# Two heads' score products on the two row halves of TensorE's array, with the forget-gate sums added by a product of their own

## The reference, cut to what matters

```python
log_f = jax.nn.log_sigmoid(f_logit.astype(jnp.float32) + b_forget[l].astype(jnp.float32))
cum = jnp.cumsum(log_f, axis=1).transpose(0, 2, 1)
...
for q0 in range(0, S, Q_BLOCK):          # Q_BLOCK = 128, S = 512, 8 heads of 64 channels
    q1 = q0 + Q_BLOCK
    s = jnp.einsum('bhqd,bhkd->bhqk', q[:, :, q0:q1], k[:, :, :q1]).astype(jnp.float32) * scale
    if cum is not None:
        s = s + cum[:, :, q0:q1, None] - cum[:, :, None, :q1]
    mask = jnp.concatenate([jnp.ones((Q_BLOCK, q0), dtype=bool), diag_mask], axis=1)
    s = jnp.where(mask, s, -jnp.inf)
    p = jax.nn.softmax(s, axis=-1).astype(v.dtype)
    outs.append(jnp.einsum('bhqk,bhkd->bhqd', p, v[:, :, :q1]))
```

## Time and profile before

| what | us |
|---|---|
| median of 3 runs (1755.65 to 1756.67) | 1756.38 |
| the profiled execution, its own time | 1755.61 |
| its span in the trace | 1753.6 |
| TensorE matmul records busy | 1727.1 (98%) |
| TensorE weight loads busy | 1375.6 (78%) |
| VectorE busy | 1088.2 (62%) |
| ScalarE busy | 685.6 (39%) |
| GpSimd busy | 197.7 (11%) |

### The profile page before, as it was taken

How to read it: one execution, slowest core, us unless ns; L and a number is a source line. 1 busy time by engine, 2 the same in 40 slices (tenths; PEclk the granted TensorE clock), 3 DMA queues, 4 the chain that set the end, 5 groups by cost and what they waited for, 6 DMA issues and landing times.

```text
span 1753.6 us, 21973 instructions
## 1 busy us (share of the span) xinstructions
PE 1727.1 (98%) x7814; PEld 1375.6 (78%) x7814; DVE 1088.2 (62%) x1646; ACT 685.6 (39%) x1130; POOL 197.7 (11%) x136
## 2 busy tenths in 40 slices
PE   7999999999999999999999999999999999999998
PEld 6777777877788888888878777777778888888886
DVE  6899987766545555533349988866755555555222
ACT  5555554433343322222236554552434423332222
POOL 1720100010030000001134310000101200000010
PEclk9999999999999999999999999999999999999999
DMA  5341211333333333333342321213333333333331
GB/s 151 91 105 50 61 49 36 96 86 94 108 96 96 96 96 96 96 90 96 90 100 64 97 60 49 55 42 103 91 96 108 96 96 96 96 96 93 94 93 69
DMA packets 310004, 152.19 MB, mean 87 GB/s; under 512 B 30436, under 2 KB 309214, under 8 KB 309932
## 3 DMA queue, kind: packets, MB, share of 16 engines
q1 hardware_dynamic: 309624, 150.99, 30.7%
q10 hardware_dynamic: 308, 0.25, 0.1%
HBM read 149.09 MB, written 2.10 MB: 86 GB/s over the span
## 4 chain that ended last, share of the span: by engine, by line
PE 93%; DVE 4%; ACT 1%; issue 1%; DMA 0%; ACTq 0%; SPq 0%; DVEq 0%; POOLq 0%
PE bank L1407 71%; PE bank L1484 12%; PE bank L1465 4%; PE bank L1517 2%; PE bank L1496 2%; DVE w_lo L979 1%; ACT w_hi L649 0%; PE bank L1648 0%; DMA x_rows<-in_x 0%; PE bank L1432 0%; DVE oc_lo L1006 0%; PE bank L1556 0%; DVE c_acc L1290 0%; DVE c_acc L1297 0%; ACT ln_sig L878 0%
## 5 line engine op out<-in xcount | busy, mean ns | idle before, releaser
L649 ACT CAST w_hi<-raw 128x1024 fp32r<-128x1024 f32 (+4 forms) x330 | 301.7, 918 | 738.8 <-PE bank L1407 737.8
L979 DVE TENSOR_TENSOR w_lo<-raw,w_hi 128x1024 fp32r<-128x1024 f32 (+4 forms) x330 | 354.2, 1076 | 224.7 <-ACT w_hi L649 223.3
L1407 PE MATMUL bank<-h_hi,w_hi 128*128 128x512 f32 (+1 forms) x1200 | 473.7, 395 | 6.9 <-DVE w_lo L979 6.6
L1407 PE MATMUL bank<-h_hi,w_lo 128*128 128x512 f32 (+1 forms) x1200 | 468.1, 390 | 0.0
L1407 PE MATMUL bank<-h_lo,w_hi 128*128 128x512 f32 (+1 forms) x1200 | 467.8, 390 | 0.0
L1407 PEld LDWEIGHTS bank<-h_hi,w_hi 128*128 128x128 f32 (+1 forms) x1200 | 225.1, 188 | 65.1 <-DVE w_lo L979 10.2
L1407 PEld LDWEIGHTS bank<-h_hi,w_lo 128*128 128x128 f32 (+1 forms) x1200 | 224.9, 187 | 48.5
L1407 PEld LDWEIGHTS bank<-h_lo,w_hi 128*128 128x128 f32 (+1 forms) x1200 | 225.2, 188 | 47.9 <-issue 2.0
L1000 DVE TENSOR_TENSOR tmp<-bank,rstd_x 128x512 f32<-128x512 f32 x140 | 96.7, 690 | 266.6 <-PE bank L1407 258.2
L1039 DVE SCALAR_TENSOR_TENSOR c_acc<-u_pad,dwk_l,c_acc 128x512 f32<-128x512 f32 x240 | 179.7, 770 | 1.2
L537 POOL TENSOR_TENSOR x_acc<-x_acc,x_sq 128x512 f32<-128x512 f32 x31 | 53.5, 1726 | 865.3 <-ACT x_sq L659 533.2
(11 more groups left out here) (221 smaller groups left out, 2152.4 us busy)
## 6 DMA issues: line engine op xcount, KB each, us to landing
raw<-in_w_in SPq DMA_DIRECT2D x96, 512.0 KB, 3.7
raw<-in_w_ffn_gate SPq DMA_DIRECT2D x44, 512.0 KB, 3.7
raw<-in_w_ffn_up SPq DMA_DIRECT2D x44, 512.0 KB, 3.7
raw<-in_w_ffn_down SPq DMA_DIRECT2D x32, 512.0 KB, 3.7
raw<-in_w_out SPq DMA_DIRECT2D x16, 512.0 KB, 3.8
raw<-in_w_ffn_down SPq DMA_DIRECT2D x16, 384.0 KB, 3.3
raw<-in_w_bo_a SPq DMA_DIRECT2D x16, 256.0 KB, 2.7
raw<-in_w_bo_b SPq DMA_DIRECT2D x16, 256.0 KB, 2.7
```

Of the source, the lines that this page charges most:

```text
L649: last = nc.scalar.copy(to, of)
L979: last = nc.vector.tensor_tensor(to, of, part.bitcast(F32), ALU.subtract)
L1407: ins = nc.tensor.matmul(bank_t[0:rows, :], wt[slot][:, w], x, start=first and k == 0 and p == 0, stop=last and k == k_tiles - 1 and p == 2)
```

## The change

The steps of the forgetting attention go by a new order, query tile by query tile, the two heads next to each other: s = 0 to 7 are head 0 and 1 of query tile 0, then of tile 3, of tile 1 and of tile 2. `p_b` gets places to match. Queries and keys of a pair stay in one 128-partition tile (head 0 on partitions 0 to 63, head 1 on 64 to 127) and are put down by one instruction. At every odd index of its loop TensorE issues the scores of two steps: two 64-row products in two banks, then two products that add the gate sums, then the two masks. The gate-sum product has 40 rows a head, 0 to 39 and 64 to 103: `cum_x` holds the sums' fp32r-rounded part in eight rows and what rounding left in eight more, 32 partitions further, zeros between, and `head_of` picks the head's two rows with the factor 1. GpSimd builds both between the chunk masks and the rotary sums. The rows of ones, the row copies by DMA and their waits go. `f_sum` moves to another place, `head_of` lies in `tmp[3]`.

```diff
@@ constants
-CUM_LOADS = {8: 0, 10: 1, 13: 2, 15: 3}
+FOX_ORDER = ((0, 0, 0), (1, 0, P), (0, 3, 2 * P), (1, 3, 6 * P), (0, 1, 0), (1, 1, 2 * P), (0, 2, 4 * P), (1, 2, 7 * P))
+CUM_ROWS = 32 + HEADS
+def step_of(g):
+    pair, s = g // 8, g % 8
+    return (pair, s // 4, s % 4, P_AT[s % 4]) if pair < PAIRS else (pair, *FOX_ORDER[s])
@@ sync (called between the loads of the fed weights, at CUM_LOADS)
-            def keys(l, pair):
-                sp.wait_ge(cum_ready, l + 1)
-                sp.wait_ge(score_done, l * STEPS + 8 * (pair + 1))
-                sp.dma_start(k_t[NOPE:NOPE + 1, 2 * pair:2 * pair + 2, :],
-                             f_sum[2 * ROPE + 2 * pair:2 * ROPE + 2 * pair + 2, :]).then_inc(cum_put[pair], 16)
@@ gpsimd, between the chunk masks and the rotary sums
+                pool.wait_ge(mask_put, 2 * TT * (l + 1))
+                if l == 0:
+                    nc.gpsimd.tensor_scalar(cum_x[:], ident[:].unsqueeze(1).broadcast_to([P, TT, P]), 0.0, None, ALU.mult).then_inc(cum_zero, 1)
+                    pool.wait_ge(cum_zero, 1)
+                    nc.gpsimd.memset(head_col[:], 0.0).then_inc(cum_zero, 1)
+                    pool.wait_ge(cum_zero, 2)
+                    for n in range(4):
+                        first = 32 * n + n // 2
+                        nc.gpsimd.tensor_copy(head_col[32 * n:32 * n + HEADS, :],
+                                              ident[32 * n:32 * n + HEADS, first:first + HEADS:2]).then_inc(cum_zero, 1)
+                        pool.wait_ge(cum_zero, 3 + n)
+                pool.wait_ge(cum_ready, l + 1)
+                passed(pool)
+                for e in range(2):
+                    nc.gpsimd.tensor_copy(cum_x[64 * e:64 * e + HEADS, :], f_sum[F, :]).then_inc(cum_hi, 1)
+                    pool.wait_ge(cum_hi, 2 * l + 1 + e)
+                nc.gpsimd.tensor_copy(head_of[:], head_col[:].unsqueeze(2).broadcast_to([P, PAIRS, P])).then_inc(cum_put, 1)
+                pool.wait_ge(cum_put, 3 * l + 1)
+                for e in range(2):
+                    nc.gpsimd.tensor_tensor(cum_x[64 * e + 32:64 * e + CUM_ROWS, :], f_sum[F, :], cum_x[64:64 + HEADS, :].bitcast(F32),
+                                            ALU.subtract).then_inc(cum_put, 1)
+                    pool.wait_ge(cum_put, 3 * l + 2 + e)
@@ gpsimd, between the pairs
-                        pool.wait_ge(score_done, score.add(8))
-                        nc.gpsimd.memset(q_t[NOPE:NOPE + 1, 2 * pair:2 * pair + 2, :], 1.0).then_inc(ones_put, 1)
-                        pool.wait_ge(ones_put, op.add())
@@ vector, put
+                    elif kind == "q":
+                        evacuated(nc.vector.scalar_tensor_tensor(q_t[:, 2 * pair, :], from_bank[:], FOX_SCALE, rstd_x[:], ALU.mult, ALU.mult))
                     else:
-                        for e in range(2):
...
+                        evacuated(nc.vector.tensor_tensor(k_t[:, 2 * pair, :], from_bank[:], rstd_x[:], ALU.mult))
@@ vector, steps
                 for g in range(STEPS):
+                    n, pair, q = g % 4, g // 8, step_of(g)[2]
+                    norm_first = pair >= PAIRS and g % 2 == 0
+                    if norm_first:
+                        normalise(g - 1)
                     dve.wait_ge(score_done, score.add())
                     ...
-                    if g:
+                    if g and not norm_first:
                         normalise(g - 1)
@@ tensor
+                def fox_logits(g):
+                    pair, q = g // 8 - PAIRS, step_of(g)[2]
+                    if g % 8 == 0:
+                        pe.wait_ge(evac_done, fed + FEED.index(f"k{pair}") + 1)
+                        pe.wait_ge(cum_put, 3 * (l + 1))
+                    ex.add()
+                    pe.wait_ge(exp_done, ex.add())
+                    w = (q + 1) * P
+                    b = [s_bank[score_slot(g + e)] for e in range(2)]
+                    for e in range(2):
+                        rows = slice(NOPE * e, NOPE * (e + 1))
+                        nc.tensor.matmul(b[e][:, 0:w], q_t[rows, 2 * pair, q * P:w], k_t[rows, 2 * pair, 0:w], start=True, stop=True)
+                    for e in range(2):
+                        rows = slice(64 * e, 64 * e + CUM_ROWS)
+                        nc.tensor.matmul(b[e][:, 0:w], head_of[rows, pair, :], cum_x[rows, 0:w], start=False, stop=True, skip_group_check=True)
+                    for e in range(2):
+                        nc.tensor.matmul(b[e][:, q * P:w], ident_b[:], mask_b[:], start=False, stop=True,
+                                         skip_group_check=True).then_inc(score_done, 1)
+                def logits(g):
+                    if g < STEPS // 2:
+                        latent_logits(g)
+                    elif g % 2:
+                        fox_logits(g - 1)
```

More of the change, by code:

```diff
@@ L352, in trunk @@
         cum_ready = sem("cum_ready")
-        cum_put = [sem(f"cum_put{i}") for i in range(PAIRS)]
+        cum_zero = sem("cum_zero")
+        cum_hi = sem("cum_hi")
+        cum_put = sem("cum_put")
         kr_ready = sem("kr_ready")
@@ L527, in _ @@
             sq, zero, stat = Count(DT), Count(), Count()
-            score, pv, evac, fed, ohi, ol = Count(), Count(), Count(EVAC_CREDIT), Count(DT), Count(O_CREDIT), Count(O_CREDIT)
-            own, fz, rt, op = Count(), Count(), Count(), Count()
+            pv, evac, fed, ohi, ol = Count(), Count(EVAC_CREDIT), Count(DT), Count(O_CREDIT), Count(O_CREDIT)
+            own, fz, rt = Count(), Count(), Count()
             def clear(acc):
@@ L556, in _ @@
             nc.gpsimd.memset(u_pad[:, :, 0:TAPS - 1], 0.0).then_inc(zero_ok, 1)
-            for l in layers([(sq, SQUARES), (zero, 5), (stat, 6), (score, STEPS), (pv, HEADS),
-                                      (evac, EVACS), (fed, FEEDS), (ohi, HEADS), (ol, HEADS), (own, 2), (fz, 1), (rt, 2), (op, PAIRS)]):
+            for l in layers([(sq, SQUARES), (zero, 5), (stat, 6), (pv, HEADS),
+                                      (evac, EVACS), (fed, FEEDS), (ohi, HEADS), (ol, HEADS), (own, 2), (fz, 1), (rt, 2)]):
                 pool.wait_ge(stat_done, stat.add())
@@ L1450, in attention, with latent_logits @@
                 units = [(n, k) for n in range(len(FEED) + 1) for k in range(DT)]
[L1452 to L1457, removed]
-                        pe.wait_ge(ones_put, op.add())
-                        pe.wait_ge(cum_put[pair % PAIRS], 16 * (l + 1))
-                    rows = (NOPE + ROPE + TT, NOPE + 1)[kind]
+                def latent_logits(g):
+                    _, e, q, _ = step_of(g)
+                    head, rows, w = 2 * (g // 8) + e, NOPE + ROPE + TT, (q + 1) * P
+                    pe.wait_ge(exp_done, ex.add())
+                    nc.tensor.matmul(s_bank[score_slot(g)][:, 0:w], q_t[0:rows, head, q * P:w], k_t[0:rows, head, 0:w],
+                                     start=True, stop=True).then_inc(score_done, 1)
@@ L1461, in logits @@
+                def fox_logits(g):
[4 more added lines that the diff above has]
+                    ex.add()
                     pe.wait_ge(exp_done, ex.add())
                     w = (q + 1) * P
-                    b = s_bank[score_slot(g)]
-                    ins = nc.tensor.matmul(b[:, 0:w], q_t[0:rows, head, q * P:w], k_t[0:rows, head, 0:w], start=True, stop=True)
@@ L1577, in _ @@
             for l in layers([(lo, CHUNKS), (ev, EVACS), (ea, 8), (fl, FEEDS), (sqa, SQUARES), (std, 5), (ex, STEPS),
-                                    (nm, STEPS), (to, STEPS), (pairs_in, HEADS), (vr, 8), (taps, CT * TAPS), (rp, HEADS), (krp, 4), (op, PAIRS)]):
+                                    (nm, STEPS), (to, STEPS), (pairs_in, HEADS), (vr, 8), (taps, CT * TAPS), (rp, HEADS), (krp, 4)]):
                 chunk(0, h, fresh=True, first_x=(l == 0))
```

47 lines of the change are left out of this document (16 added, 31 removed).

## The result

The kernel after takes 1765.65 us, the median of 4 runs (1765.37 to 1767.57), against 1756.02 of before in the same measurement (1755.31 to 1756.67): a ratio of 1.0059 with a 95% interval of 1.0047 to 1.0071. It is slower by 9.6 us, where 1752.4 was forecast, and lies outside the range. The profiled executions differ as much: 1765.55 against 1755.61, +9.9. Some executions of the changed versions run at a slightly lower mean clock and take 2 to 3 us longer (the profiled ones among them, e7 and e8, show the granted clock at about one half near 128 us); the two profiled executions just named show 1.00 there.

What follows compares the result with a forecast made beforehand. TensorE's summed work was taken to bound the attention. Score steps save 4.3 us and norm waits cost 0.3, so 4.0 off the 1756.38 median gives 1752.4 us; its own range was 1747 to 1755, the wider range 1747 to 1760.

Steps and rivals of the forecast that it cites:

- The sum for a step: A pair's score step on TensorE: 0.50 + 4w/2400 + 0.23w/512 us for w keys; 4.70 against 5.24 us a pair, 4.3 saved over eight.
- the upper bound of four: Narrow fp32r gate-sum passes at four clocks a column, no faster than fp32; gives back 1.2 us for 128 keys alone.
- its 0.3: TensorE waits for VectorE's norms at step 40 and a few like steps: 0.3 us for both layers.
- (a): Score products of the two row halves don't overlap but run one behind another: 17.4 us slower, 1774; 13%.
- (b): Partial overlap: head 1's first score pass starts only with head 0's second; 8.5 us in all, say 1758; 10%.
- (c): Weight loads of the two row halves go one after another: 4 to 5 us, no change, 1756.5; 15%.
- hidden with 4 to spare: GpSimd's new gate work ahead of the rotary sums: 7.1 us, hidden under 11.2 us of cover.
- Rival (d): GpSimd's gate work overruns 11.2 us, or VectorE's norms wait in many steps: 3 to 14 us back, 1760; 7%.
- Nothing there: Unchanged rest: the product behind the values loses its weights' lead as before, now a feed product bears it; no cost.
- 4.3 - 0.3 = 4.0 us off: Whole kernel: score-step saving less norm waits, put on the median of 1756.38 to give 1752.4 us.

Runs made afterwards that it cites:

- e7: After with arrays from `r0` on 128 bytes further than before, products ordered score 0, sums 0, score 1, sums 1: 1767.72 us, ratio 1.0063.
- e8: After with arrays from `r0` on 128 bytes further than before, each head's mask directly behind its own sums: 1798.31 us, ratio 1.0242.
- e9: After with `head_col` laid out behind the last array, so all shared arrays lie where before has them: 1756.81 us, ratio 1.0005.
- e6: After with arrays from `r0` on 128 bytes further than before, GpSimd's gate work behind the rotary sums: 1767.59 us, ratio 1.0072.
- e10: As e9, with the two subtractions for the low rows of `cum_x` on VectorE instead of GpSimd: 1753.37 us, ratio 0.9986.
- e4: Before with only `f_hi` and `f_lo`, the down products' operands, 32 bytes further: 1763.05 us, ratio 1.0041.
- e2: Before with only 32 unused bytes behind `f_sum`, moving `r0` 32 bytes further: 1768.05 us, ratio 1.0070.
- e14: Before with weight tiles `w_hi` and `w_lo` 32 bytes further and the arrays behind them 256 further: 1789.56 us, ratio 1.0196.
- e3: Before with 64 unused bytes behind `f_sum`, moving `r0` 64 bytes further: 1760.37 us, ratio 1.0024.
- e11: Before with 128 unused bytes behind `f_sum`, moving `r0` 128 bytes further: 1766.57 us, ratio 1.0062.

## Why the prediction was wrong, by its own steps

**The sum for a step: right.** 1.56 and 0.75 measured for 1.58 and 0.77, 0.58 saved a pair for 0.54, 4.4 us in all for 4.3. The split into entering, loads, columns, masks and leaving was tested only by its sum at two widths. The narrow gate-sum passes can be read from the difference of the two steps: 1.47 - 0.66 = 0.81 us for 384 columns. Four clocks a column for the scores are 0.64 of it, and the 0.17 left is one clock a column for the sums; by the upper bound of four it would be 0.64.

**VectorE: its work fell, its 0.3 was not seen.** VectorE is busy for 1077.5 us instead of 1088.2, and no TensorE wait for a norm falls in the forgetting attention of after.

**Rivals (a), (b), (c): fell.** (a) and (b) by the two passes within a hundredth of a us and by e7, where even the order issued did not hold the second head back; e8 shows that a product over all rows does. The Trainium skill's 3.07 for four row tiles (TensorE: Matmul & The Clock Gate, Measured speedup vs the span model), which the prediction set beside its own size of (b), did not carry over to two tiles in this kernel: their passes cost no more than one head's. (c) fell because the 128-key step, where serial loads would have shown most, is 0.02 below the forecast.

**GpSimd: the step "hidden with 4 to spare" failed, in a way it did not ask about.** The queue was hidden, with 6.6 to spare. The prediction priced the new work as time on GpSimd and never as time taken from VectorE, which runs beside it, splits the weights that TensorE wants next and carries the path to the rotary sums. That is 2.44 us in layer 0 and 0.8 in layer 1 (e9, in the layout of before, has 2.41 and 0.78), shown by the rows above, by e6 (the slowing moves with the work) and by e10 (it shrinks as the work leaves). Rival (d) named the outcome but a different mechanism, an overrun. The Trainium skill has the rule (SBUF — State Buffer, Who interferes with whom): a VectorE instruction with two SBUF inputs contends with a GpSimd instruction that reads SBUF. The trace agrees for the taps and for `u_pad`; a weight split of 0.95 us that starts at 100.83, with GpSimd's first casts beside it, is not slowed, so the rule does not size every case.

**The unchanged rest: "Nothing there", and the sum "4.3 - 0.3 = 4.0 us off", failed.** This is the step that decides the miss. The prediction had no term for the dense products, since none of their instructions is touched. They lost 11.2 us to where the new 16-byte array was put: about 7.3 in the two down products (e4), the rest in the other products whose streamed tile lies behind `r0`, most of whose mean records are 4 to 7 ns longer in after; those of `f_hi` are 6 longer (391 to 397). The layout is not the whole miss: e9, free of it, has a median of 1756.81 and not 1752.4. There the late starts take 3.2 us, and eight of 11 executions the 2 to 3 us of the lower clock, which no term of the prediction had either.

**The closed sum**, in profiled executions: -4.4 (steps) + 2.4 + 0.8 (late starts) + 11.2 (layout, after less e9) = +10.0, and +9.9 is measured. Since the 11.2 is itself a difference to e9, this tests the other three terms: without it they give -1.2, and e9's profiled execution measures 1754.35 - 1755.61 = -1.3. The two traces give the layout a second way. From the first dense pass behind layer 0's attention to the first score of layer 1 after takes 683.54 for 677.13 us, 6.4 more, of which 0.8 is the late start; from the first dense pass behind layer 1's attention to the end of the span it takes 591.42 for 585.66, 5.8 more: 11.4 in all. For e10, -4.4 + 1.3 + 0.5 = -2.6, measured 1753.02 - 1755.61 = -2.6.

**Open.** Why the distance matters: weight loads and streamed reads run at the same time, and a collision of the two would fit, but no run looked at it. Why it costs 12.3 us in before (e2) and 11.2 in after. Why e14 costs less than its passes were expected to. Why the clock falls in some executions and not in others.

## What to carry to other kernels

Before costing an edit, list the arrays that it adds and whether any array behind them moves; a diff that touches no dense product can slow all of them, and a padded copy of the old kernel (e2) shows that in one run. Compare passes in a fixed stretch of untouched work, ahead of any look at the changed work. And cost a helper engine's new work twice: once as its own queue, once as what it does to the engine that runs beside it; a stretch of the old trace where the two already run together gives the price.

## What the runs showed of the hardware

- The rate of 512-column fp32r passes that each load new weights depends on the distance between streamed tile and weight tile: 178 passes in 40 us at the distance of before and 256 bytes from it, 176 at 64 (e3), 173 at 32 (e2) and at 128 (e11), at the same granted clock.
- Score passes of two row halves start together even when the first head's gate-sum product stands between them in program order (e7). A product over all rows between them separates the heads, for about 1 us a step, each head's own loads, masks and changes of form included (e8).
- While GpSimd's subtractions of 8 partitions ran, VectorE's instructions over 128 partitions took nearly twice their time: 4.36 for 2.33 (three taps), 2.31 for 1.22 (a split).
- In some executions TensorE's clock fell to half behind the stall ahead of the attention. Busy time in e7, where TensorE worked 3.06 of 5 us and was granted 0.50 for the next 3:

```profile
123.00:128.00 5.00, 3.06 (x18) 2.31 (x16) 3.98 (x4) 3.95 (x7) 4.85 (x3) 1.00 0.67 178
128.00:131.00 3.00, 2.67 (x9) 2.46 (x10) 1.47 (x4) 0.95 (x3) 0.01 (x1) 0.50 0.16 48
```

In e9's profiled execution TensorE worked even less, 2.49 of the same 5 us, and stayed at 1.00, so the stall alone does not decide it.
